# Eight PSUM banks in the head and VectorE for the residual's scaling, with a reordered router stage

## The chip, the cores and the metric

The kernel runs on 1 core of one Trainium2 chip. The metric is the device time of one execution in microseconds (us), lower is better. Three runs of the kernel before gave 830.20, 831.35 and 834.64 us; the median is 831.35.

## The reference

One layer over 16 learned meta tokens and 512 real tokens of width 1024. All matrix products are float32-exact to the tolerance, which the kernel reaches with three reduced products per float32 one.

```python
h = layer_norm(concat(meta_tokens, x), ln_in_g, ln_in_b)          # 528 x 1024
p = h @ w_in                                                      # all projections
(q_m, k_m, v_m, o_m, i_pre, f_pre, q_a, c_kv, q_idx, k_idx, w_idx, g_m, g_a) = split(p)
h_m = head_norm(mlstm(silu(conv(q_m, k_m)), v_m, i_pre, f_pre)) * mnorm_g * sigmoid(o_m)
h_a = sparse_attention(q_a, rms_norm(c_kv), q_idx, k_idx, w_idx)  # top 128 keys per query
y = sigmoid(g_m) * (h_m @ w_branch_m) + sigmoid(g_a) * (h_a @ w_branch_a)
h = layer_norm(2**0.25 * h + y @ w_out, ln1_g, ln1_b)
scores = sigmoid(h @ w_router)                                    # 16 experts, 4 groups
# best group by its top two scores, the two best experts of it, normalised weights
moe = sum over chosen e: weight * (silu(h @ w_gate[e]) * (h @ w_up[e])) @ w_down[e]
return layer_norm(2**0.25 * h + moe, ln2_g, ln2_b)[:, 16:]
```

## The kernel before, in words

Every engine has one hand-written instruction stream; the streams meet only in counting semaphores (`q[...]`), and an engine works its stream strictly in order. A step helper adds a wait of an engine on its own instruction.

A float32 operand is split into a high part (ScalarE, a copy to float32r) and a low part (VectorE, the difference), and `product` (lines 1066 to 1068) issues high x high, high x low and low x high. Weights come in 1 MB units: SyncE loads a unit into one of three `raw` slots, ScalarE's `split_hi` (line 681) and VectorE's `split_lo` (line 1582) split it. In the expert stage the same is done with twelve `m_raw` slots and three split slots (`m_split_hi` line 938, `m_split_lo` line 1864).

**The head.** SyncE issues the relative-bias table and a one-hot matrix, then the four token tiles `xn`, the meta tile `xm`, the gains `lng`, `lnb`, and weights. TensorE first multiplies the table by the one-hot matrix (lines 1097, 1098) into PSUM, ScalarE copies it out to `ftab` and stores it. VectorE takes means and variances per tile (lines 1596 to 1598), GpSimd the power (line 545), ScalarE normalises (line 690). TensorE transposes (line 1104) four of the eight 128-column groups `c` of each tile into banks 4 to 7; the other four groups (line 1110) follow later, each when the bank of group `c - 4` has been emptied (`lo_x`). Per group, ScalarE and VectorE apply gain and shift and make the two parts: for even `c` ScalarE writes `tmpT` (line 703) and the high part (705), for odd `c` ScalarE writes the high part straight from PSUM (698) and VectorE makes `tmpT` (1612); VectorE makes the low part (1613). The meta tile goes the same way in one piece (lines 1114, 1616, 1617, 707, 1619). The projections start when both parts of everything are there:

```python
pe.wait_ge(q["hi_x"], KC + 1)
pe.wait_ge(q["lo_x"], KC + 1)
```

**The residual.** The normalised tokens are also wanted later, with gain and bias, in token layout. GpSimd multiplies `xn` by the broadcast gain `gbc` and adds `bbc` (lines 566, 567), tile by tile, once all ten late loads (`load_late`, of which `kvg` is the last issued) and all transposes are through; SyncE stores each tile (line 424) and only then loads weight unit 4. ScalarE waits for all four stores before it squares the latent keys (line 729, whose output tile `md` lies on `xn`'s memory).

**The first projections.** TensorE works, in order, unit 0 (lines 1066 to 1068, twice 528 tokens), one half of unit 1, transposes of the latent keys (line 1148), the other half of unit 1, then a wait for VectorE's `c_tok` (line 1631) before four small transposes (line 1153) and unit 2. `c_tok` needs the squares (729), VectorE's `css` (1624), GpSimd's power and, in VectorE's order, `split_lo(2)`.

**The router stage.** After the output projection, tile `i` of `h1` is normalised by VectorE (line 1885), transposed by TensorE (`turned(i)`, line 1386), copied out by ScalarE (line 949) and multiplied by the router's weights (`router(i)`, line 1393). TensorE's order is `router(0), turned(2), router(1), turned(3), router(2), router(3)`. ScalarE splits `m_hi` units 0 and 1 before it copies tile 3 out. Then ScalarE's sigmoid (line 964), VectorE's choice of experts (lines 1898 to 1924), ranks (line 1421), lists (lines 1951, 1461), a gather of the first expert's tokens by GpSimd, its transposition (line 1441, all eight groups, `xe_done`), the split in `xe_hi` (ScalarE, line 970) and `xe_lo` (VectorE, line 1929), and the first expert's units.

In both kernels the loop over experts and the closing stage are the same.

## Time and profile before

| | |
|---|---|
| median of three runs | 831.35 us |
| the profiled execution's own time | 831.14 us |
| its span, first to last instruction | 829.1 us |
| what lies around the span | 2.0 us |
| TensorE busy | 760.9 us, 92% of the span |
| VectorE busy | 591.1 us, 71% |
| ScalarE busy | 431.7 us, 52% |
| GpSimd busy | 100.3 us, 12% |
| granted TensorE clock, mean | 0.970 |

The span is the time from the first to the last instruction on the core. Busy shares are means over stages with different limits, so each stage has to be read by itself. PE is TensorE, PEld its weight load, DVE VectorE, ACT ScalarE, POOL GpSimd, SPq and ACTq the instructions of SyncE and ScalarE that issue DMAs.

### The profile page before, as it was taken

To read this page: it belongs to the slowest core of one execution; us is meant where nothing else is said; L and a number is where in the kernel's file an instruction comes from. 1 tells how busy PE (TensorE), PEld (TensorE's weight loads), DVE (VectorE), ACT (ScalarE), POOL (GpSimd) and SP (SyncE) were. 2 spreads that over 40 slices of the span, in tenths; PEclk is the share of its full clock that TensorE was granted. 3 is DMA by queue.
4 is the path that set the end of the run, shared out by engine and by line. 5 is a ranking of instruction groups with operands and counts; after the bars stand their busy time and mean duration, and the time that the engine had idled before them with its cause. 6 is when DMAs were issued, how large, how long until landed. Compare 5 with 4: busy or idle time off the path is not lost.

```text
span 829.1 us, 10885 instructions
## 1 busy us (share of the span) xinstructions
PE 760.9 (92%) x4024; PEld 612.9 (74%) x4026; DVE 591.1 (71%) x797; ACT 431.7 (52%) x506; POOL 100.3 (12%) x116
## 2 busy tenths in 40 slices
PE   3399999999899899999999868899999999999993
PEld 1296799897467577787888766688888888888872
DVE  4905999797226644542464867889898989898978
ACT  4433333343642544573232032577888777878745
POOL 5540000000001000000000201212111111112001
PEclk9999999999999899999999977999999999999997
DMA  8645222321055111135237973799999999999162
GB/s 201 202 131 195 89 84 70 103 58 44 0 180 220 61 52 52 51 106 171 81 104 257 407 251 106 254 328 409 399 398 397 395 399 396 391 402 397 61 249 102
DMA packets 102469, 171.09 MB, mean 206 GB/s; under 512 B 18760, under 2 KB 39496, under 8 KB 102368
## 3 DMA queue, kind: packets, MB, share of 16 engines
q1 hardware_dynamic: 95672, 151.82, 51.5%
q0 software_dynamic: 4608, 12.92, 4.0%
q10 hardware_dynamic: 2152, 5.85, 1.8%
q8 instruction: 24, 0.39, 0.2%
q14 instruction: 13, 0.11, 0.0%
HBM read 160.26 MB, written 21.09 MB: 219 GB/s over the span
## 4 chain that ended last, share of the span: by engine, by line
PE 83%; DVE 9%; issue 3%; ACT 3%; SPq 1%; DMA 1%; POOL 0%; DVEq 0%; ACTq 0%; POOLq 0%
PE low L1066 15%; PE low L1068 15%; PE low L1067 15%; PE wide L1066 7%; PE wide L1068 7%; PE wide L1067 7%; PE wide L1441 2%; PE low L1236 1%; PE low L1336 1%; PE low L1298 1%; PE wide L1221 1%; PE low L1393 1%; PE wide L1269 1%; PE wide L1454 1%; SPq L407 1%
## 5 line engine op out<-in xcount | busy, mean ns | idle before, releaser
L1864 DVE TENSOR_TENSOR m_lo<-m_raw,m_hi 128x2048 fp32r<-128x2048 f32 x95 | 215.0, 2290 | 30.9 <-ACT m_hi L938 30.2
L938 ACT ACTIVATE m_hi<-m_raw 128x2048 fp32r<-128x2048 f32 x95 | 179.8, 1918 | 24.8 <-PE low L1068 24.0
L1066 PE MATMUL low<-m_hi,xe_hi 128*128 128x512 f32 x256 | 103.4, 404 | 2.6 <-DVE xe_lo L1929 1.5
L1066 PE MATMUL low<-hT_hi,w_hi 128*128 128x512 f32 (+1 forms) x240 | 95.6, 398 | 10.6 <-issue 10.6
L1068 PE MATMUL low<-m_hi,xe_lo 128*128 128x512 f32 x256 | 100.7, 393 | 0.0
L1067 PE MATMUL low<-m_lo,xe_hi 128*128 128x512 f32 x256 | 100.2, 392 | 0.0
L1582 DVE TENSOR_TENSOR w_lo<-raw,w_hi 128x2048 fp32r<-128x2048 f32 x28 | 64.1, 2290 | 45.7 <-ACT w_hi L681 45.5
L1067 PE MATMUL low<-hT_lo,w_hi 128*128 128x512 f32 (+1 forms) x240 | 93.4, 389 | 0.0
L1068 PE MATMUL low<-hT_hi,w_lo 128*128 128x512 f32 (+1 forms) x240 | 92.7, 386 | 0.0
L681 ACT ACTIVATE w_hi<-raw 128x2048 fp32r<-128x2048 f32 x28 | 53.5, 1910 | 17.6 <-PE wide L1068 8.3
L1066 PEld LDWEIGHTS low<-hT_hi,w_hi 128*128 128x128 f32 x240 | 46.8, 195 | 20.3 <-issue 11.0
L1066 PEld LDWEIGHTS low<-m_hi,xe_hi 128*128 128x128 f32 x256 | 48.5, 189 | 15.7 <-DVE m_lo L1864 4.4
L1068 PEld LDWEIGHTS low<-m_hi,xe_lo 128*128 128x128 f32 x256 | 48.3, 189 | 10.7
L1067 PEld LDWEIGHTS low<-m_lo,xe_hi 128*128 128x128 f32 x256 | 48.6, 190 | 9.3
L1068 PEld LDWEIGHTS low<-hT_hi,w_lo 128*128 128x128 f32 x240 | 46.8, 195 | 9.2
L1067 PEld LDWEIGHTS low<-hT_lo,w_hi 128*128 128x128 f32 x240 | 46.9, 195 | 8.6 <-issue 0.2
L1066 PE MATMUL wide<-m_hi,hd_hi 128*128 128x512 f32 x128 | 51.4, 402 | 1.4 <-DVE hd_lo L1938 1.4
L1068 PE MATMUL wide<-m_hi,hd_lo 128*128 128x512 f32 x128 | 50.1, 391 | 0.0
L1067 PE MATMUL wide<-m_lo,hd_hi 128*128 128x512 f32 x128 | 49.8, 389 | 0.0
L970 ACT ACTIVATE xe_hi<-wide 128x1024 fp32r<-128x1024 f32 x16 | 16.4, 1027 | 45.5 <-PE wide L1441 45.5
L1066 PE MATMUL wide<-hT_hi,w_hi 128*128 128x264 f32 x128 | 36.9, 288 | 1.1 <-ACT relu L759 1.0
L1067 PE MATMUL wide<-hT_lo,w_hi 128*128 128x264 f32 x128 | 36.3, 283 | 0.0
(370 smaller groups left out, 1465.8 us busy)
## 6 DMA issues: line engine op xcount, KB each, us to landing
m_raw<-in_w_gate SPq DMA_DIRECT2D x32, 1024.0 KB, 8.9
m_raw<-in_w_up SPq DMA_DIRECT2D x32, 1024.0 KB, 8.3
m_raw<-in_w_down SPq DMA_DIRECT2D x31, 1024.0 KB, 9.5
raw<-in_w_in SPq DMA_DIRECT2D x19, 1024.0 KB, 5.3
raw<-in_w_out SPq DMA_DIRECT2D x4, 1024.0 KB, 5.0
y<-y_dram SPq DMA_DIRECT2D x8, 512.0 KB, 6.9
table_dram<-table_row ACTq DMA_DIRECT2D x1, 2624.0 KB
strips<-table_dram SPq DMA_DIRECT2D x8, 264.0 KB, 4.3
```

The costliest lines, as they stand in the source:

```text
L407: sp.dma_start(unit3(raw, u % RAW, u)[:, :, to:to + n], src).then_inc(raw_loaded[u % RAW], 16)
L681: nc.scalar.activation(w_hi[:, u % SPL, :], raw[:, u % RAW, :], ACT.Copy).then_inc(q["hi_ready"], 1)
L938: nc.scalar.activation(m_hi[n % MS][:, :], (m_spare if is_last(n, j) else m_raw[slot])[:, :], ACT.Copy).then_inc(q["m_hi_ready"], 1)
L970: nc.scalar.activation(xe_hi[:, :, :], wide[1][:, :].rearrange("p (c x) -> p c x", c=KC), ACT.Copy).then_inc(q["xe_hi_ready"], 1)
L1066: nc.tensor.matmul(outp, lh, rh, start=first, stop=False)
L1067: nc.tensor.matmul(outp, lh, rl, start=False, stop=False)
L1068: return nc.tensor.matmul(outp, ll, rh, start=False, stop=last)
L1221: mm = nc.tensor.matmul(o, kT[:, h, META + j * P:META + (j + 1) * P], qT[:, h, META + j * P:T], start=True, stop=True)
L1236: mm = nc.tensor.matmul(oo, dw[:, g % 2, lo:lo + P], v_ext[:, j, g, :], start=False, stop=(j == i))
L1441: mm = nc.tensor.transpose(wide[1][:, c * P:(c + 1) * P], xg[slot][:, c * P:(c + 1) * P], ident[:, :])
L1582: v.tensor_tensor(w_lo[:, u % SPL, :], raw[:, u % RAW, :], w_hi[:, u % SPL, :].bitcast(F32), ALU.subtract).then_inc(q["lo_ready"], 1)
L1864: v.tensor_tensor(m_lo[n % MS][:, :], (m_spare if is_last(n, j) else m_raw[n % MR])[:, :], m_hi[n % MS][:, :].bitcast(F32), ALU.subtract). ...
```

## The change

**Head.** The table product, its copy and its store move from the front to after unit 1 (ScalarE copies it out before `split_hi(3)`); the loads of table and one-hot matrix move behind the first weights and the two broadcast rows. All eight groups of each tile are transposed at once, into banks 4, 5, 6, 7, 0, 1, 2, 3; the meta tile's transposes go to bank 4 after `lo_x` is 1. ScalarE does groups 0 and 1 before `split_hi(0)`. GpSimd builds two masks between the powers of the first tiles. The eight scaling instructions go from GpSimd to VectorE, after `split_lo(1)`. ScalarE's squares write into `score` and no longer wait for the stores. `side_done` and `side_out` replace six signals (`kv_done`, `ckv_done`, `table_done`, and `kv_out`, `fabs_ready`, `table_out`) and count to three each.

**Router stage.** `turned(2)` goes ahead of `router(0)`; a float32 product of 512 columns whose result nobody reads follows `router(0)` and `turned(3)`; unit 1's two splits go behind the sigmoid (ScalarE) and behind `slots_of(2, 8)` (VectorE); the split of the first expert's tokens is done in two halves of 512 columns, and the first expert unit waits for the first half only.

```diff
 (SyncE)
-            sp.dma_start(relb[:, :], a["rel_bias"]).then_inc(q["table_in"], 16)
-            sp.dma_start(oneh[:, :], onehot).then_inc(q["table_in"], 16)
             for i in range(TT):
                 sp.dma_start(xn[:, i, :], a["x"][0, i * P:(i + 1) * P, :]).then_inc(x_loaded[i], 16)
...
             load(1)
+            sp.dma_start(gbc[:, :], bcast_rows(a["ln_in_g"], D)).then_inc(q["load_late"], 16)
+            sp.dma_start(bbc[:, :], bcast_rows(a["ln_in_b"], D)).then_inc(q["load_late"], 16)
+            sp.dma_start(relb[:, :], a["rel_bias"]).then_inc(q["table_in"], 16)
+            sp.dma_start(oneh[:, :], onehot).then_inc(q["table_in"], 16)
...
-            sp.dma_start(gbc[:, :], bcast_rows(a["ln_in_g"], D)).then_inc(q["load_late"], 16)
-            sp.dma_start(bbc[:, :], bcast_rows(a["ln_in_b"], D)).then_inc(q["load_late"], 16)
 (GpSimd)
-            pool.wait_ge(q["load_late"], 16 * 10)
-            pool.wait_ge(q["xt_done"], KC)
-            for i in range(TT):
-                pool.wait_ge(q["xn_ready"], i + 1)
-                step(nc.gpsimd.tensor_tensor(xn[:, i, :], xn[:, i, :], gbc[:, :], ALU.mult))
-                nc.gpsimd.tensor_tensor(xn[:, i, :], xn[:, i, :], bbc[:, :], ALU.add).then_inc(q["h_ready"], 1)
-                pool.wait_ge(q["h_ready"], i + 1)
 (ScalarE)
-            act.wait_ge(q["table_done"], 1)
-            nc.scalar.activation(ftab[:, :], wide[0][0:AH, 0:FX], ACT.Copy).then_inc(q["table_out"], 1)
-            act.wait_ge(q["table_out"], 1)
-            act.dma_start(table_row, ftab[:, :]).then_inc(q["table_put"], 16)
...
-            split_hi(0)
             act.wait_ge(q["load_consts"], 16 * 2)
             for c in range(KC):
+                if c == 2:
+                    split_hi(0)
                 act.wait_ge(q["xt_done"], c + 1)
...
-            act.wait_ge(q["h_stored"], 16 * TT)
...
-                square = nc.scalar.activation(md[0:n, 0:R], src, ACT.Square, accum_out=css[0:n, i:i + 1])
+                square = nc.scalar.activation(score[0:n, 0:R], src, ACT.Square, accum_out=css[0:n, i:i + 1])
...
             evac(B_QI + 1, qidxT[:, 1, :])
+            act.wait_ge(q["side_done"], 3)
+            nc.scalar.activation(ftab[:, :], wide[0][0:AH, 0:FX], ACT.Copy).then_inc(q["side_out"], 1)
+            act.wait_ge(q["side_out"], 3)
+            act.dma_start(table_row, ftab[:, :]).then_inc(q["table_put"], 16)
             split_hi(3)
+            act.wait_ge(q["h_stored"], 16 * TT)
...
             m_split_hi(0)
-            m_split_hi(1)
             store_h1(3)
             turned_out(3)
...
+            m_split_hi(1)
             m_split_hi(MS - 1)
...
-            xe_hi_out(0)
+            act.wait_ge(q["xe_done"], 1)
+            for half, done in ((0, "xe_half_hi"), (1, "xe_hi_ready")):
+                nc.scalar.activation(xe_hi[:, 4 * half:4 * half + 4, :], bank[6 + half][:, :].rearrange("p (c x) -> p c x", c=4), ACT.Copy).then_inc(q[done], 1)
 (TensorE)
             for i in range(TT):
                 pe.wait_ge(q["xn_ready"], i + 1)
-                for c in range(4):
-                    mm = nc.tensor.transpose(bank[4 + c][:, i * P:(i + 1) * P], xn[:, i, c * P:(c + 1) * P], ident[:, :])
+                for c in range(KC):
+                    mm = nc.tensor.transpose(bank[(4 + c) % 8][:, i * P:(i + 1) * P], xn[:, i, c * P:(c + 1) * P], ident[:, :])
                     if i == TT - 1:
                         mm.then_inc(q["xt_done"], 1)
-            for c in range(4, KC):
-                pe.wait_ge(q["lo_x"], c - 3)
...
             by_channel(take(B_QI + 1)[:, :], 1, P, META, T).then_inc(q["block_done"], 1)
+            pe.wait_ge(q["table_in"], 32)
+            nc.tensor.matmul(wide[0][0:AH, 0:512], relb[:, :], oneh[:, 0:512], start=True, stop=True)
+            nc.tensor.matmul(wide[0][0:AH, 512:FX], relb[:, :], oneh[:, 512:FX], start=True, stop=True).then_inc(q["side_done"], 1)
             pe.wait_ge(q["c_ready"], TT + 1)
...
+            def idle_product():
+                nc.tensor.matmul(bank[1][:, :], ident[:, :], g1[:, 0:512], start=True, stop=True)
             pe.wait_ge(q["late_consts"], 16 * 8)
+            turned(2)
             router(0)
-            turned(2)
+            idle_product()
             router(1)
             turned(3)
+            idle_product()
             router(2)
             router(3)
...
-            pe.wait_ge(q["xe_lo_ready"], 1)
             for u in range(4):
+                pe.wait_ge(q["xe_lo_ready" if u else "xe_half_lo"], 1)
 (VectorE)
             split_lo(1)
+            dve.wait_ge(q["load_late"], 16 * 10)
+            for i in range(TT):
+                step(v.tensor_tensor(xn[:, i, :], xn[:, i, :], gbc[:, :], ALU.mult))
+                v.tensor_tensor(xn[:, i, :], xn[:, i, :], bbc[:, :], ALU.add).then_inc(q["h_ready"], 1)
             dve.wait_ge(q["css_ready"], 1)
...
-            for u in range(MS - 1):
-                m_split_lo(u)
+            m_split_lo(0)
...
             slots_of(2, 8)
+            m_split_lo(1)
             m_split_lo(MS - 1)
-            xe_lo_out(0)
+            for half, ready, done in ((0, "xe_half_hi", "xe_half_lo"), (1, "xe_hi_ready", "xe_lo_ready")):
+                dve.wait_ge(q[ready], 1)
+                v.tensor_tensor(xe_lo[:, 4 * half:4 * half + 4, :], bank[6 + half][:, :].rearrange("p (c x) -> p c x", c=4),
+                                xe_hi[:, 4 * half:4 * half + 4, :].bitcast(F32), ALU.subtract).then_inc(q[done], 1)
```

## Rows read from the trace of the kernel before

**Rows 1.** The page: the chain that ended last, by engine.
```profile
PE 83%; DVE 9%; issue 3%; ACT 3%; SPq 1%; DMA 1%; POOL 0%; DVEq 0%; ACTq 0%; POOLq 0%
```
**Rows 2.** Waits of TensorE, whole span: who waited for whom, us, times, longest.
```profile
PE low L1066 <- issue: 10.6, 1, 10.6
PE low L1153 <- DVE c_tok L1631: 2.0, 1, 2.0
PE low L1448 <- DVE hid L1934: 1.5, 1, 1.5
```
**Rows 3.** Timeline of VectorE, 26 to 42 us: start, duration, instruction, count, idle before.
```profile
26.42 1.50 DVE L1613 TENSOR_TENSOR hT_lo<-tmpT,hT_hi 128x512 fp32r<-128x512 f32 x2
28.74 3.44 DVE L1613 TENSOR_TENSOR hT_lo<-tmpT,hT_hi 128x512 fp32r<-128x512 f32 x2
32.94 1.99 DVE L1613 TENSOR_TENSOR hT_lo<-tmpT,hT_hi 128x512 fp32r<-128x512 f32 x1
34.85 0.28 DVE L1616 TENSOR_TENSOR tmpM<-low,lng 128x128 f32<-128x128 f32 x1
35.16 2.11 DVE L1617 TENSOR_TENSOR tmpM<-tmpM,lnb 128x128 f32<-128x128 f32 x1
37.65 2.05 DVE L1619 TENSOR_TENSOR hT_lo<-tmpM,hT_hi 128x128 fp32r<-128x128 f32 x1 [0.38 <-ACT hT_hi L707]
39.62 2.28 DVE L1582 TENSOR_TENSOR w_lo<-raw,w_hi 128x2048 fp32r<-128x2048 f32 x1
```
**Rows 4.** Timeline of GpSimd, 28 to 52 us.
```profile
29.19 2.44 POOL L566 TENSOR_TENSOR xn<-xn,gbc 128x1024 f32<-128x1024 f32 x1 [8.38 <-DMA kvg<-in_kv_norm_g]
39.63 4.50 POOL L566 TENSOR_TENSOR xn<-xn,gbc 128x1024 f32<-128x1024 f32 x1
```
**Rows 5.** Timeline of the head, 0 to 40 us, all engines.
```profile
0.81 0.40 SPq L395 DMA_DIRECT2D relb<-in_rel_bias  x1
1.72 1.94 SPq L398 DMA_DIRECT2D xn<-in_x  x4
10.77 1.09 PE L1104 MATMUL wide<-ident,xn 128*128 128x128 f32 x4 [5.00 <-ACT xn L690]
17.38 1.91 ACT L681 ACTIVATE w_hi<-raw 128x2048 fp32r<-128x2048 f32 x1 [1.80 <-DMA raw<-in_w_in]
19.20 0.76 ACT L703 ACTIVATE tmpT<-wide,lnb,lng 128x512 f32<-128x512 f32 x1
19.99 0.63 ACT L705 ACTIVATE hT_hi<-tmpT 128x512 fp32r<-128x512 f32 x1
20.53 0.76 ACT L698 ACTIVATE hT_hi<-wide,lnb,lng 128x512 fp32r<-128x512 f32 x1
39.80 0.56 PE L1066 MATMUL low<-hT_hi,w_hi 128*128 128x264 f32 x1 [10.56 <-issue]
```
**Rows 6.** Timeline of VectorE, after the head.
```profile
62.14 0.17 DVE L1624 TENSOR_SCALAR css<-css 128x4 f32<-128x4 f32 x1 [20.24 <-ACT md L729]
```
**Rows 7.** Windows: stretch and length, busy us per engine (count), granted clock, DMA share, GB/s.
```profile
68.00:72.00 4.00, 4.00 (x11) 3.12 (x12) 3.86 (x5) 0.01 (x1) 0.00 (x0) 0.58 0.93 298
72.00:76.00 4.00, 4.00 (x18) 3.25 (x18) 3.75 (x5) 0.60 (x1) 0.00 (x0) 0.99 0.53 199
469.00:473.00 4.00, 1.49 (x14) 1.25 (x13) 3.44 (x5) 0.44 (x1) 1.46 (x1) 1.00 1.04 411
484.60:491.20 6.60, 6.50 (x34) 6.39 (x32) 4.31 (x3) 2.44 (x3) 0.00 (x0) 0.53 0.69 247
```
**Rows 8.** The chain of waits in the router stage: start, length, instruction, count.
```profile
478.79 1.69 PE low L1393 x16
484.80 6.32 PE low L1393 x32
```
**Rows 9.** Timeline of VectorE before the first expert's units.
```profile
510.43 1.22 DVE L1929 TENSOR_TENSOR xe_lo<-wide,xe_hi 128x1024 fp32r<-128x1024 f32 x1 [2.96 <-ACT xe_hi L970]
```
**Rows 10.** The chain of waits in the closing stage.
```profile
805.69 1.72 PE wide L1558 x4
```

More of the change, by code:

```diff
@@ L546, in _ @@
                 pool.wait_ge(q["rstd_ready"], i + 1)
+                if i == 0:
+                    step(nc.gpsimd.memset(tri_qs[:, :], 0.0))
+                    step(nc.gpsimd.affine_select(out=tri_qs[:, :], in_=tri_qs[:, :], compare_op=ALU.is_ge, fill=NOT_CAUSAL,
+                                                 base=0, pattern=[[-1, P]], channel_multiplier=1))
+                elif i == 1:
+                    step(nc.gpsimd.memset(tri_st[:, :], 0.0))
+                    step(nc.gpsimd.affine_select(out=tri_st[:, :], in_=tri_st[:, :], compare_op=ALU.is_ge, fill=NEG_MASK,
+                                                 base=0, pattern=[[1, P]], channel_multiplier=-1))
             for h in range(MH):
                 step(nc.gpsimd.tensor_copy(sel_row[64:68, h, :], ident[64:68, 64 + h:65 + h].to_broadcast([MH, P])))
-            step(nc.gpsimd.memset(tri_qs[:, :], 0.0))
-            step(nc.gpsimd.affine_select(out=tri_qs[:, :], in_=tri_qs[:, :], compare_op=ALU.is_ge, fill=NOT_CAUSAL,
-                                         base=0, pattern=[[-1, P]], channel_multiplier=1))
-            step(nc.gpsimd.memset(tri_st[:, :], 0.0))
-            step(nc.gpsimd.affine_select(out=tri_st[:, :], in_=tri_st[:, :], compare_op=ALU.is_ge, fill=NEG_MASK,
-                                         base=0, pattern=[[1, P]], channel_multiplier=-1))
             step(nc.gpsimd.memset(mask[:, 0:P], 0.0))
@@ L702, in _ @@
                     act.wait_ge(q["lo_x"], c - 1)
-                step(nc.scalar.activation(tmpT[:, c % 2, :], bank[4 + c % 4][:, :], ACT.Identity,
+                step(nc.scalar.activation(tmpT[:, c % 2, :], bank[(4 + c) % 8][:, :], ACT.Identity,
                                           bias=lnb[:, c:c + 1], scale=lng[:, c:c + 1]))
@@ L714, in _ @@
             act.wait_ge(q["block_out"], 1)
-            act.wait_ge(q["kv_done"], 1)
-            nc.scalar.activation(in_halves(cT[:, :]), both_halves(low[1][:, :]), ACT.Copy).then_inc(q["kv_out"], 1)
+            act.wait_ge(q["side_done"], 1)
+            nc.scalar.activation(in_halves(cT[:, :]), both_halves(low[1][:, :]), ACT.Copy).then_inc(q["side_out"], 1)
             act.wait_ge(q["load_late"], 16 * 10)
@@ L720, in _ @@
             step(nc.scalar.activation(rows[96:100, 0, :], rows[96:100, 0, :], ACT.Exp, scale=-1.0))
-            nc.scalar.activation(rows[96:100, 0, :], rows[96:100, 0, :], ACT.Ln, bias=1.0).then_inc(q["fabs_ready"], 1)
-            act.wait_ge(q["ckv_done"], 1)
+            nc.scalar.activation(rows[96:100, 0, :], rows[96:100, 0, :], ACT.Ln, bias=1.0).then_inc(q["side_out"], 1)
+            act.wait_ge(q["side_done"], 2)
             act.wait_ge(q["const_done"], 1)
-            act.wait_ge(q["h_stored"], 16 * TT)
             for i in range(TT + 1):
@@ L1094, in by_token @@
                 return mm
-            pe.wait_ge(q["table_in"], 32)
-            nc.tensor.matmul(wide[0][0:AH, 0:512], relb[:, :], oneh[:, 0:512], start=True, stop=True)
-            nc.tensor.matmul(wide[0][0:AH, 512:FX], relb[:, :], oneh[:, 512:FX], start=True, stop=True).then_inc(q["table_done"], 1)
-            pe.wait_ge(q["table_out"], 1)
             pe.wait_ge(q["const_done"], 1)
@@ L1120, in _ @@
             all_tokens(low[0], 0, 0).then_inc(q["block_done"], 1)
-            all_tokens(low[1], 0, R).then_inc(q["kv_done"], 1)
+            all_tokens(low[1], 0, R).then_inc(q["side_done"], 1)
             def channel_unit(u, b):
@@ L1156, in _ @@
             pe.wait_ge(q["block_out"], B_QI + 2)
+            pe.wait_ge(q["side_out"], 3)
             index_scores(0)
@@ L1611, in _ @@
                         dve.wait_ge(q["lo_x"], c - 1)
-                    step(v.tensor_scalar(tmpT[:, 1, :], bank[4 + c % 4][:, :], lng[:, c:c + 1], lnb[:, c:c + 1], ALU.mult, ALU.add))
+                    step(v.tensor_scalar(tmpT[:, 1, :], bank[(4 + c) % 8][:, :], lng[:, c:c + 1], lnb[:, c:c + 1], ALU.mult, ALU.add))
                 v.tensor_tensor(hT_lo[:, c, META:T], tmpT[:, c % 2, :], hT_hi[:, c, META:T].bitcast(F32), ALU.subtract).then_inc(q["lo_x"], 1)
@@ L1615, in _ @@
             wide_c = lambda t: t[:, :].rearrange("p (c o) -> p c o", o=1).to_broadcast([P, KC, META])
-            step(v.tensor_tensor(tmpM[:, :, :], bank[2][:, 0:KC * META].rearrange("p (c x) -> p c x", c=KC), wide_c(lng), ALU.mult))
+            step(v.tensor_tensor(tmpM[:, :, :], bank[4][:, 0:KC * META].rearrange("p (c x) -> p c x", c=KC), wide_c(lng), ALU.mult))
             v.tensor_tensor(tmpM[:, :, :], tmpM[:, :, :], wide_c(lnb), ALU.add).then_inc(q["affine_m"], 1)
```

25 lines of the change are left out of this document (11 added, 14 removed).

## The prediction

> **What bounds the kernel now.** I read first the chain that ended last: TensorE has 83% of it, VectorE 9% [rows 1]. So a change pays only where TensorE stands still or runs slowly. The waits of TensorE then say where: one of 10.6 us before the first projection, put down to "issue" because two VectorE and ScalarE signals end it together, 2.0 us for `c_tok`, 1.5 us for the first expert's `hid` [rows 2]. The first is by far the longest, and everything after it hangs on it: the projections begin at 39.80 [rows 5].
>
> What fills the head is in the timelines of VectorE and GpSimd side by side. An `hT_lo` difference takes 0.75 us (two in 1.50). From 28.74 on, two take 3.44 and the last takes 1.99; the add into `tmpM` over 128 columns takes 2.11 and the last `hT_lo`, as small, 2.05, where its neighbour L1616, which reads one operand from PSUM, takes 0.28 [rows 3]. These stretched ones lie in the time in which GpSimd scales the residual, from 29.19 on [rows 4]. The reverse is there too: at 39.62 VectorE's `w_lo` starts first and takes its plain 2.28, and GpSimd's product, begun at 39.63, takes 4.50 instead of 2.44 [rows 3, 4]. The two engines take turns for whole instructions when both have two operands in SBUF. The granted clock of TensorE comes last: 0.58 from 68 to 72 us and 0.53 from 484.6 to 491.2 [rows 7], at 1.2 GHz for most of both.
>
> **The head.** Four terms.
> (a) Two loads leave SyncE's front. The first token tile was issued at 1.72 and can go at 0.81 [rows 5]: 0.9 us. The statistics are VectorE's own back to back work behind the first tile, so all of it moves.
> (b) Order of the first groups. The first tile's transposes start at 10.77 - 0.9 = 9.9. Now there are 32 of them ahead of the end, four in 1.09 [rows 5], so 0.27 each, and the last tile's eight begin at 9.9 + 24 x 0.27 = 16.4; group 0 is whole at 16.7. ScalarE does groups 0 and 1 (0.76 + 0.63 + 0.76, 2.2 with gaps) to 18.9 and then splits unit 0 (1.91) to 20.8, whose weights had landed at 17.4 [rows 5] and come no later. VectorE's `w_lo` (2.28) ends at 23.1. Before, ScalarE split first, from 17.38, did groups 0 and 1 to 21.3, then VectorE made group 1's 0.8 + 0.75 and `w_lo` to about 25.0. So VectorE passes this point 1.9 us earlier, the 0.9 of (a) included.
> (c) From there VectorE and ScalarE pass the groups back and forth as before. Without GpSimd's instructions beside them the stretched ones fall to their plain length: 3.44 to 1.50, 1.99 to 0.75, 2.11 to 0.28, 2.05 to 0.28: 1.9 + 1.2 + 1.8 + 1.8 = 6.7 us. GpSimd keeps memsets, copies and masks, over before 20 us.
> (d) The eight banks take the waits of the later transposes away; they were no longer than VectorE's own queue, so nothing more. The meta tile's transposes wait for group 0 alone: nothing.
> Head: 1.9 + 6.7 = 8.6 us; the first projection starts at 31.2. Bounds: 7.5 (one of the slow instructions has another reason) to 9.5 (transposes faster, below).
>
> The Trainium skill, SBUF — State Buffer, section "Who interferes with whom", says that a VectorE instruction with two SBUF inputs and a GpSimd instruction that reads SBUF exclude each other for the whole instruction, and that one with at most one SBUF input isn't held. The 0.28 beside the 2.11 [rows 3] agrees. By that rule only GpSimd's own reading counts: (c) would be whole, and the eight scaling instructions on VectorE hold nobody, since GpSimd then has nothing to read.
>
> **What moves into cover.** VectorE's scaling: eight instructions of 128x1024. `w_lo` has twice the columns and takes 2.28 [rows 3], so 1.14 plus 0.1 for the step: 10 us. They stand behind `split_lo(1)` (31.2 + 1.9 for the high part + 2.3 = 35.4), so they last to 45.4. Behind them in VectorE's queue is `css`, for which VectorE stood idle 20.24 us until 62.14 [rows 6]; 8.6 earlier that is 53.5. So 8 us are left, and they cost nothing. If the cover were gone, each us would be one of `c_tok` and of TensorE. Their own wait, for all ten late loads, ended at 29.19 before [rows 4] and is in time; the order change in SyncE's queue (two rows ahead, two small loads more) adds under 1 us to it. SyncE stores the four tiles by about 48.5 and then loads unit 4, some 3.5 us sooner than before: nothing. ScalarE's squares don't wait for the stores; they waited for TensorE's transposes before, so nothing. The table's product on TensorE (656 columns; 512 take 0.86, two in 1.72 [rows 10], so 1.1 us) falls in the 2.0 us in which TensorE waits for `c_tok` [rows 2]: `c_tok` comes from ScalarE and VectorE and keeps its distance, so the product costs nothing and 0.9 us of waiting is left. ScalarE's copy of it (0.7) and the wait for its store stand before unit 3's high part and before `qaT`; both have some 5 us of idle time there. Bound if not: 0.7 us. Six signals on two counters: no instruction less, nothing.
>
> **The clock after `c_tok`.** After the 2.0 us of waiting, the clock fell and 11 products ran between 68 and 72 where 18 run between 72 and 76 [rows 7]: 7 products of 0.22, 1.6 us lost. With 0.9 us of idle time and a product before it, I expect the clock to stay: 1.6 us won. Against it: at 469 to 473 TensorE worked only 1.49 of 4.00 us and the clock stayed at 1.00 [rows 7], so whether it falls depends on more than the length of one pause. Bounds 0 and 1.7. I take 1.6.
>
> **The router stage.** TensorE from 478.8: `turned(2)` 1.1 (eight transposes at the full clock take what four do at half), `router(0)` 1.7 [rows 8], idle product 0.86 [rows 10], `router(1)` 1.7, `turned(3)` 1.1, at 485.2; the second idle product to 486.1; `router(2)` and `router(3)` 1.7 each to 489.5. ScalarE's copy of tile 3, now in front of unit 1's split, is ready 1.1 after 485.2 and isn't waited for. Before: 484.80 + 6.32 = 491.12, since the last 32 records ran at half clock (16 took 1.69 before, 32 take 6.32 [rows 8]). So 1.6 won if the clock stays to the end; if it falls where it fell before, the second idle product takes 1.7 and the sum is 485.2 + 1.7 + 6.3 = 493.2: 2.1 lost. I think that it stays through the idle products and falls late in the last 3.4 us: 1.2 won.
> Behind it VectorE gets 2.3 us more before the first expert's tokens (unit 1's low part); it stood idle 2.96 us there [rows 9], so it's hidden, with 0.6 left. The halves: before, 1.03 for the high part and 1.22 for the low [rows 9], 2.3 in all. Now the first half is ready after 0.6 + 0.7, so TensorE starts 1.0 sooner; but VectorE, whose queue then ends in `hid`, for which TensorE waits 1.5 [rows 2], is through only 0.2 sooner (0.6 + 0.6 + 0.1 + 0.7 against 2.3). So 0.2 counts. Bounds of the stage: -2.1 and +2.6. Taken: 1.2 + 0.2 = 1.4. Unit 1's slot comes free some 17 us later, and its reload with it; a slot's contents are used more than 30 us after, so nothing.
>
> **Sum.** 8.6 + 1.6 + 1.4 = 11.6 us off the profiled execution's own 831.1 (span 829.1 and 2.0 around it): 819.5. The median of the runs shown is 831.35, so the two are one scale. I forecast 819.5, 1.4% faster. The experts and the closing stage start earlier and are otherwise as before: TensorE is busy through and pulls its weights along.
>
> **Rivals.**
> 1. The clock gives nothing at either place: 8.6 + 0.2 us: 822.3. For it: the fall in rows 7 has a pause that is only halved, and the router's products are short. 0.22.
> 2. The transposes warm TensorE. The 32 of the head follow each other without a pause for 8.7 us, and the projections from 39.80 reach the full rate after some microseconds of work. If they do so too, the last tile's are ready 0.8 us sooner, and with everything else as forecast 818.7. 
> 3. The stretched VectorE rows have another cause than GpSimd (the broadcast loads of `gbc`, `bbc` land at that time): then only 1.9 + 1.6 + 1.4 is won less 1 for the same slowness in the scaling: 827.2. Against it: the 0.28 between two stretched rows and GpSimd's 4.50. 0.05.
> 4. A later stage takes it back: from 100 to 200 us VectorE's top-k selection is nearly as full as TensorE, and a pause falls at a worse moment for the clock several times. Each fall costs 1.6 us; four of them and a us of waiting give 826. 0.06.
> 5. Slower than before: VectorE's scaling stands in front of `css`. It decides once the last late load lands after 43.5; each us later is one us for `c_tok`, the projections and all behind. To eat the 11.6 it has to land at 55 or later, at 60 the time is 836. The load's neighbours in SyncE's queue landed by 29.19 [rows 4]. 0.03.
> Forecast: 0.52.
>
> **How the numbers follow.** Changes of this kernel within 0.5% (4.2 us) can't be told from none: faster means under 827.2. Forecast, 1, 2 and half of 4 are faster: 0.89. Rival 3 and half of 4: 0.08 the same. Rival 5: 0.03. The range: the forecast's own goes from 8.6 + 1.6 + 2.6 with 0.8 and a us of noise (816) to a head of 7.5 with nothing from the clock (823.6). That also covers rivals 1 and 2; 816 to 823.6 leaves out rivals 3 to 5 and little else.
>
> **What would show it.** Right: the first L1066 product at 31.2, every L1613 at 0.7 to 0.8 and L1617, L1619 at 0.3; eight 1.2 us instructions on VectorE and `css` still preceded by idle time; 0.9 us before the `smallT` transposes and 0.23 between the products of unit 2; the sigmoid's idle time ended at a distance of 11 us from the end of the output projection instead of 12.5, and a granted clock near 1 until 486 minus the head's gain. Wrong: slow small VectorE instructions with GpSimd idle; `css` without idle time before it; a clock of 0.5 from `turned(3)` on; a first projection after 33 us, which would cost the forecast most.

## The result, and the profile after

The changed kernel takes 818.86 us (median of 4 runs, 816.62 to 819.72) against 830.78 for the kernel before in the same job (828.96 to 834.64): a ratio of 0.985, 95% interval 0.981 to 0.989. The forecast was 819.5 us, with a range of 816.0 to 823.6. The profiled execution took 818.94 us, of which 817.2 are its span, so 12.2 us less than the one of before.

The chain that ended last, by engine (answers to [rows 1]):
```profile
PE 84%; DVE 10%; ACT 3%; issue 2%; DMA 0%; POOL 0%; DVEq 0%; ACTq 0%; POOLq 0%
```
TensorE is still the bound. Its waits (engine, tile, line, what it waited for, us, times, longest; answers to [rows 2]):
```profile
PE low L1061 <- DVE hT_lo L1617: 11.2, 1, 11.2
...
PE low L1061 <- DVE m_lo L1865: 1.7, 1, 1.7
...
PE low L1446 <- DVE hid L1934: 1.5, 1, 1.5
```
The wait before the first projection is no shorter than before (11.2 against 10.6), since the transposes in front of it end sooner too. The length of a wait doesn't show the gain; its end does. VectorE's timeline shows that end (start, duration, instruction, count, idle before; answers to [rows 3] and [rows 6]):
```profile
4.21 1.42 DVE L1594 BATCH_NORM_STATS2 stats<-xn 128x6 f32<-128x512 f32 x2 [4.21 <-DMA xn<-in_x]
...
19.16 2.29 DVE L1580 TENSOR_TENSOR w_lo<-raw,w_hi 128x2048 fp32r<-128x2048 f32 x1 [0.26 <-ACT w_hi L675]
...
25.13 1.44 DVE L1611 TENSOR_TENSOR hT_lo<-tmpT,hT_hi 128x512 fp32r<-128x512 f32 x2
...
27.39 0.69 DVE L1611 TENSOR_TENSOR hT_lo<-tmpT,hT_hi 128x512 fp32r<-128x512 f32 x1
28.00 0.28 DVE L1614 TENSOR_TENSOR tmpM<-wide,lng 128x128 f32<-128x128 f32 x1
28.32 0.29 DVE L1615 TENSOR_TENSOR tmpM<-tmpM,lnb 128x128 f32<-128x128 f32 x1
28.98 0.29 DVE L1617 TENSOR_TENSOR hT_lo<-tmpM,hT_hi 128x128 fp32r<-128x128 f32 x1 [0.38 <-ACT hT_hi L697]
...
32.99 1.22 DVE L1621 TENSOR_TENSOR xn<-xn,gbc 128x1024 f32<-128x1024 f32 x1
...
41.42 1.22 DVE L1622 TENSOR_TENSOR xn<-xn,bbc 128x1024 f32<-128x1024 f32 x1
52.18 0.17 DVE L1625 TENSOR_SCALAR css<-css 128x4 f32<-128x4 f32 x1 [9.54 <-ACT score L718]
```
Every stretched row is down to its plain length, and the eight scaling instructions (32.99 to 42.64) are followed by 9.5 us of idle time: they lie in cover. TensorE's timeline of the head (answers to [rows 5]):
```profile
9.37 1.09 PE L1095 MATMUL wide<-ident,xn 128*128 128x128 f32 x4 [9.37 <-ACT xn L679]
10.25 1.06 PE L1095 MATMUL low<-ident,xn 128*128 128x128 f32 x4
...
14.80 0.64 PE L1095 MATMUL wide<-ident,xn 128*128 128x128 f32 x4
15.28 0.60 PE L1095 MATMUL low<-ident,xn 128*128 128x128 f32 x4
...
29.37 0.56 PE L1061 MATMUL low<-hT_hi,w_hi 128*128 128x264 f32 x1 [11.21 <-DVE hT_lo L1617]
29.73 0.42 PE L1062 MATMUL low<-hT_lo,w_hi 128*128 128x264 f32 x1
```
Four transposes take 1.06 to 1.11 until the last tile, whose four take 0.60 to 0.64: TensorE has risen to 2.4 GHz while it did nothing but transposes. (The durations say so. The column of the granted clock reads 1.00 from the start of the trace to its first fall and can't be used here.) The projections then start 0.22 apart, at 1.2 GHz again after 11.2 us of idle time.

Around `c_tok`, the same engine (the wait of 2.0 us in [rows 2]):
```profile
55.54 1.02 PE L1139 MATMUL wide<-oneh,relb 32*8 32x512 f32 x2
56.41 0.40 PE L1140 MATMUL wide<-oneh,relb 32*8 32x144 f32 x2
57.62 0.41 PE L1143 MATMUL low<-ident,smallT 8*128 8x8 f32 x4 [0.81 <-DVE c_tok L1632]
...
59.62 0.63 PE L1061 MATMUL low<-hT_hi,w_hi 128*128 128x512 f32 x1
```
The table product fills the wait and 0.81 is left. But the products from 59.2 to 62.6 are 0.43 apart, not 0.23: the clock fell all the same. The windows say it in another way (stretch, length, busy time and count of PE, PEld, DVE, ACT, POOL, granted clock, DMA share, GB/s; answers to [rows 7]):
```profile
60.00:64.00 4.00, 4.00 (x13) 3.13 (x12) 3.79 (x7) 0.17 (x1) 0.00 (x0) 0.67 0.34 116
...
474.00:478.00 4.00, 4.00 (x33) 3.52 (x33) 2.43 (x3) 1.67 (x2) 0.00 (x0) 1.00 0.66 264
478.00:482.00 4.00, 2.00 (x15) 1.89 (x14) 1.43 (x7) 1.96 (x3) 0.00 (x0) 0.64 0.88 272
```
In the router stage it stayed at 1.00 up to 478 and fell near 479. The chain of waits there (start, length, what; answers to [rows 8]) has the idle products at L1403:
```profile
470.03 1.69 PE low L1384 x16
471.72 0.95 PE low L1403 x2
472.67 1.69 PE low L1384 x16
474.37 0.92 PE wide L1377 x8
475.28 0.86 PE low L1403 x2
476.14 3.87 PE low L1384 x32
```
The last 32 router records take 3.87 instead of 6.32 [rows 8]. And the halves of the first expert's tokens on VectorE (answers to [rows 9]), with the wait of the first unit on TensorE:
```profile
498.49 1.27 DVE L1978 TENSOR_TENSOR xe_lo<-wide,xe_hi 128x512 fp32r<-128x512 f32 x2
```
```profile
499.22 0.50 PE L1061 MATMUL low<-m_hi,xe_hi 128*128 128x512 f32 x1 [0.88 <-DVE xe_lo L1978]
...
510.45 0.47 PE L1061 MATMUL low<-m_hi,xe_hi 128*128 128x512 f32 x1 [1.71 <-DVE m_lo L1865]
```

(`xe_lo` is the low part of the expert's tokens, `m_lo` that of a weight unit.) Where the time came from, by the start of the same work in the two timelines (us from the start of each span):

| point | before | after | sooner |
|---|---|---|---|
| first projection | 39.80 | 29.37 | 10.4 |
| `smallT` transposes behind `c_tok` | 67.58 | 57.62 | 10.0 |
| first index scores | 80.82 | 70.83 | 10.0 |
| end of the output projection | 478.63 | 468.99 | 9.6 |
| sigmoid | 491.14 | 480.04 | 11.1 |
| first expert unit | 511.71 | 499.22 | 12.5 |
| first `hid` transposes | 527.71 | 515.81 | 11.9 |
| transposes of the next expert's tokens | 541.51 | 528.02 | 13.5 |
| last expert done (`yl_hi`) | 803.09 | 791.12 | 12.0 |
| end of the span | 829.1 | 817.2 | 11.9 |

### The profile page after: what moved, and what is told of

The parts are those of the page before. It is cut to its first block, busy times and chain, and to the rows that moved or that the text cites. A ratio compares the mean times of both kernels' runs of the same rounds, so it can differ in the third digit from the quotient of the medians.

```text
span 817.2 us, 10896 instructions
## 1 busy us (share of the span) xinstructions
PE 754.8 (92%) x4030; PEld 609.8 (75%) x4030; DVE 593.6 (73%) x806; ACT 431.9 (53%) x507; POOL 78.2 (10%) x108
## 4 chain that ended last, share of the span: by engine, by line
PE 84%; DVE 10%; ACT 3%; issue 2%; DMA 0%; POOL 0%; DVEq 0%; ACTq 0%; POOLq 0%
PE low L1061 15%; PE low L1062 15%; PE low L1063 15%; PE wide L1061 7%; PE wide L1063 7%; PE wide L1062 7%; PE wide L1439 1%; PE low L1227 1%; DVE slots L1951 1%; DVE m_lo L1865 1%; PE low L1327 1%; PE wide L1212 1%; PE low L1289 1%; ACT w_hi L675 1%; PE wide L1260 1%
## 5 line engine op out<-in xcount | busy, mean ns | idle before, releaser
L931 ACT ACTIVATE m_hi<-m_raw 128x2048 fp32r<-128x2048 f32 x95 | 179.6, 1917 | 23.1 <-PE low L1063 22.6
L1061 PE MATMUL low<-hT_hi,w_hi 128*128 128x512 f32 (+1 forms) x240 | 95.8, 399 | 11.2 <-DVE hT_lo L1617 11.2
L1063 PE MATMUL wide<-hT_hi,w_lo 128*128 128x264 f32 x128 | 36.2, 283 | 0.0
```

What stands on the lines that cost most here:

```text
L931: nc.scalar.activation(m_hi[n % MS][:, :], (m_spare if is_last(n, j) else m_raw[slot])[:, :], ACT.Copy).then_inc(q["m_hi_ready"], 1)
L1061: nc.tensor.matmul(outp, lh, rh, start=first, stop=False)
L1063: return nc.tensor.matmul(outp, ll, rh, start=False, stop=last)
```

## The experiments

All were timed in five rounds beside the kernel before (medians 831.56, 831.23 and 830.41 in the three jobs). `a1` is an edit of the kernel before, the others of the changed kernel. The points of the table are measured in each experiment's own profile, one per kernel.

**a1_scale_only: the kernel before with nothing but the scaling moved to VectorE.**
```diff
-            pool.wait_ge(q["load_late"], 16 * 10)
-            ... (GpSimd's loop over the tiles)
+            dve.wait_ge(q["load_late"], 16 * 10)
+            for i in range(TT):
+                step(v.tensor_tensor(xn[:, i, :], xn[:, i, :], gbc[:, :], ALU.mult))
+                v.tensor_tensor(xn[:, i, :], xn[:, i, :], bbc[:, :], ALU.add).then_inc(q["h_ready"], 1)
```

> The kernel before with one edit: the eight scaling instructions of the residual move from GpSimd to VectorE, behind the split of unit 1. Theory (the two engines exclude each other while both read two operands from SBUF): the four stretched VectorE instructions fall to 0.7 and 0.3 us, the first projection starts at 33.0 instead of 39.8, and the time is 831 - 7 = 824 us. Rival (the broadcast loads or something else stretch them): they stay at 2 us with GpSimd idle, the first projection stays at 39.8, 831 us.

Measured: 823.54 us (820.54 to 824.95), ratio 0.990 (0.987 to 0.992). VectorE's timeline:
```profile
28.91 1.44 DVE L1605 TENSOR_TENSOR hT_lo<-tmpT,hT_hi 128x512 fp32r<-128x512 f32 x2
...
31.17 0.69 DVE L1605 TENSOR_TENSOR hT_lo<-tmpT,hT_hi 128x512 fp32r<-128x512 f32 x1
31.78 0.28 DVE L1608 TENSOR_TENSOR tmpM<-low,lng 128x128 f32<-128x128 f32 x1
32.10 0.29 DVE L1609 TENSOR_TENSOR tmpM<-tmpM,lnb 128x128 f32<-128x128 f32 x1
32.77 0.29 DVE L1611 TENSOR_TENSOR hT_lo<-tmpM,hT_hi 128x128 fp32r<-128x128 f32 x1 [0.38 <-ACT hT_hi L699]
```
All four kinds of stretched rows are plain again, with every load where it was, and the first projection starts at 33.16, 6.6 us sooner. So GpSimd was the cause, not the loads beside it. Both the time and the start came out as expected.

**a2_scale_pool: the changed kernel with the scaling back on GpSimd** (the same edit the other way round).

> The changed kernel with the scaling given back to GpSimd, all else kept. My record says that the move is worth 6.7 us: then the first projection starts at about 36 and the time is 825 to 826. Rival, which the changed kernel's trace suggests: GpSimd can begin only when the last late load has landed, at about 29.3, and the reordered head is through at 29.4 by then, so only the last small instruction and the split of unit 1 can be stretched; the first projection starts at 29.4 to 31.5 and the time is 819 to 821.

Measured: 819.20 us (816.95 to 821.19), ratio 0.985 (0.983 to 0.988): the same as the changed kernel. The first projection starts at 29.56. GpSimd's and VectorE's timelines say why:
```profile
30.43 2.38 POOL L568 TENSOR_TENSOR xn<-xn,gbc 128x1024 f32<-128x1024 f32 x1 [11.41 <-DMA kvg<-in_kv_norm_g]
32.88 4.31 POOL L569 TENSOR_TENSOR xn<-xn,bbc 128x1024 f32<-128x1024 f32 x1
```
```profile
29.17 0.29 DVE L1625 TENSOR_TENSOR hT_lo<-tmpM,hT_hi 128x128 fp32r<-128x128 f32 x1 [0.38 <-ACT hT_hi L705]
30.97 3.98 DVE L1588 TENSOR_TENSOR w_lo<-raw,w_hi 128x2048 fp32r<-128x2048 f32 x1 [1.51 <-ACT w_hi L683]
```
GpSimd starts when the late loads have landed, at 30.43, and VectorE has finished the head at 29.46. The two still collide, in unit 1's `w_lo` (3.98 instead of 2.29), but TensorE's first projections don't wait for that one. (The late loads also end 1.2 us later than in the kernel before, 30.43 against 29.19, since their order was changed.) In the changed kernel, then, the move of the scaling is worth nothing, and the orders alone bring 10.2 us at the first projection. Each of the two is enough by itself to keep the head out of GpSimd's way; their gains overlap and don't add.

**a3_router_before: the changed kernel with the router stage and the first expert's tokens as before** (order of `turned` and `router`, no idle products, one split of 1024 columns, unit 1's splits back in front).

> The changed kernel with the whole router stage of the kernel before (order of transposes, no idle products, unit 1 split early, tokens split in one piece). Theory: from the end of the output projection to the sigmoid 12.5 us instead of 11.0, the granted clock 0.5 during the last two router products, and the first expert's second phase 2.3 us later by the difference of the two traces: 821.0 us. Rival (the stage gives nothing because VectorE sets the pace behind it): 819 us.

Measured: 820.47 us (819.23 to 820.92), ratio 0.987 (0.984 to 0.989). From the end of the output projection to the sigmoid 12.4 us, as before (12.5; changed kernel 11.05), and to the first expert unit 33.1 us against 30.2. At the transposes of the next expert's tokens its stage has cost 3.9 us (63.0 against 59.0); the whole span is only 1.5 longer (818.7), since its output projection ended 0.7 sooner and a later fall of the clock, told of under Rival 4 below, is missing from its profile.

**a4_no_idle: the changed kernel without the two idle products.**
```diff
             router(0)
-            idle_product()
...
             turned(3)
-            idle_product()
```

> The changed kernel without the two idle products. Theory (they hold the clock): it falls to 0.5 near the third tile's transposes, the last two router products take 6.3 us instead of 3.9, 2.4 lost and 1.7 saved: sigmoid 0.7 us later than in the changed kernel, 819.6 us. Rival (the order of transposes alone keeps the clock): both products' 1.7 us are saved, or as much of it as tile 3's wait allows, some 1 us: 818 us.

Measured: 821.47 us (819.35 to 822.72), ratio 0.988 (0.986 to 0.990). The chain of waits:
```profile
472.75 6.14 PE low L1384 x32
```
TensorE's timeline, just in front of them:
```profile
471.66 1.09 PE L1377 MATMUL wide<-ident,h 128*128 128x128 f32 x8 [0.57 <-DVE h L1884]
```
Without the idle products the last 32 records are back at 6.14, and the sigmoid comes 12.35 after the output projection, 1.3 more than in the changed kernel. So of the 1.46 gained up to the sigmoid all but 0.16 is the idle products'; the third tile's earlier turn does next to nothing alone. They do two things at once: they put wide products between the narrow ones, and they fill the 0.57 us for which TensorE waits there without them (0.61 in the kernel before). Which of the two holds the clock no run separates. I had expected 819.6 us, 1.9 less than measured. A second fall of the clock came back with it, 40 us later, in the windows of this kernel (first row) and of the changed one (second):
```profile
516.00:520.00 4.00, 3.44 (x10) 2.80 (x11) 3.66 (x4) 3.01 (x3) 0.00 (x0) 0.70 0.95 376
```
```profile
516.00:520.00 4.00, 3.44 (x17) 2.72 (x17) 3.68 (x3) 3.46 (x3) 0.31 (x1) 1.00 1.02 386
```
With as many busy us, 10 products run instead of 17, and from `hid` to the next expert's tokens it takes 1.6 longer. This went the same way in every profile of the study: 13.8 to 13.9 us from `hid` to the next tokens in all four without idle products (the kernel before, `a1`, `a3`, `a4`), 12.2 in the ten with them. How products near 473 keep the clock up at 517 no run tells. The sigmoid came 12.4 to 12.6 us after the output projection in those four and 11.05 to 11.6 in the ten, so the gain of 1.46 is the upper end of what the idle products bring.

**b4_four_banks: the changed kernel with the transposes of before** (four groups ahead, then one by one as banks come free, `bank[4 + c % 4]`).

> The changed kernel with the transposes of the kernel before: four groups per tile into banks 4 to 7, the other four groups later into the same banks, the meta tile's into bank 2. All other orders are the changed kernel's. Theory (my record's term d, the eight banks are worth nothing): the later transposes are ready before ScalarE asks for them, and group 0 is whole 0.7 us sooner since only four transposes stand ahead of it per tile; the first projection starts between 28.7 and 29.4 and the time is 818 to 819. Rival (the eight banks are what shortened the head): the first projection at 31 or later, 820.5 or more.

Measured: 816.85 us (815.46 to 822.53), ratio 0.984 (0.982 to 0.987). The first projection starts at 28.88, 0.5 sooner than in the changed kernel. ScalarE takes the first group at 14.72 instead of 15.22, since fewer transposes stand ahead of it, and everything behind keeps that distance. The eight banks bring nothing. That they cost this half us fits ScalarE's row, but the first projections of other kernels with eight banks and no edit in the head lie between 29.03 (`a3`) and 30.09 (`c4`), so 28.88 isn't clear of them. The median is more than 1 us under the range that I had expected (818 to 819).

**b1_warm_head: 19 products of 512 columns, whose result nobody reads, while TensorE waits for the head.**
```diff
+            for c, count in ((3, 8), (5, 3), (6, 3), (7, 3), (8, 2)):
+                pe.wait_ge(q["lo_x"], c)
+                for _ in range(count):
+                    nc.tensor.matmul(bank[5][:, :], hT_hi[:, 0, META:META + P], hT_hi[:, 0, META:T], start=True, stop=True)
```

> The changed kernel with 19 reduced products of 512 columns that nobody reads on TensorE in the head's last 7 us (8 once three groups have their low part, then 3, 3, 3 and 2 as the later ones come), in the pause before the first projection. Theory (the clock is low there because TensorE stood still): the first 25 or so products of 264 columns take 0.12 us instead of 0.22 and the gain is 2.3 us, 816.5. Rival (the products delay something or the clock isn't raised): 818.9 or more, the first projection later than 29.4.

Measured: 813.33 us (812.56 to 814.19), ratio 0.979 (0.977 to 0.980), the fastest of the study. TensorE's timeline:
```profile
22.09 6.79 PE L1106 MATMUL wide<-hT_hi 128*128 128x512 f32 x19 [3.85 <-DVE hT_lo L1615]
29.38 0.36 PE L1061 MATMUL low<-hT_hi,w_hi 128*128 128x264 f32 x1 [0.50 <-ACT hT_hi L697]
29.58 0.28 PE L1062 MATMUL low<-hT_lo,w_hi 128*128 128x264 f32 x1
```
The first projection starts at the same time (29.38), but the projections are 0.12 apart from the first on. The `smallT` transposes come at 54.91, 2.7 sooner. In its profile the clock stays up behind `c_tok` too, so that the first index scores are 4.3 sooner (66.57) and the span is 812.1. The median is 3.2 us under the 816.5 that I had expected. Of the 5.2 us by which the span is shorter, 2.7 are the products' own; 1.6 come from the clock behind `c_tok` and 1.6 from another fall, near 786 us, that its profile doesn't have; 0.8 are lost between the first index scores and the first expert unit. Whether the products bring the two stretches at full clock as well, or the profile met them by chance, isn't shown. And even the 2.7 depend on what is compared: from the first projection to the `smallT` transposes it takes 25.5 us with them, 28.2 in the changed kernel, but 26.9 in `a4`, `b4` and `c1`, where the clock rose sooner.

**b2_warm_ctok: three idle products behind the table product**, to fill the last 0.8 us before `c_tok`; **b3_warm_both**: both of these.

> The changed kernel with 3 reduced products of 512 columns behind the table's product, in the 0.8 us in which TensorE waits for c_tok. Theory (the pause and the narrow products around it let the clock fall at 59.3): the clock stays in more of the executions, unit 2's products take 0.23 throughout, up to 1.6 us gained, 817.3. Rival (the fall depends on when the pause meets the chip's own rhythm, not on 0.7 us of filling): 818.9, and the fall still in the trace.

> Both fillings together. Theory: the gains add, 2.3 + up to 1.6: 815 to 816.5. Rival: no better than the better of the two.

Measured: `b2` 815.36 us (811.99 to 817.48), ratio 0.980 (0.978 to 0.982); `b3` 814.81 us (812.71 to 815.19), ratio 0.980 (0.978 to 0.982). The window of `b2` that answers to the 0.67 of the changed kernel:
```profile
60.00:64.00 4.00, 4.00 (x19) 3.21 (x18) 3.87 (x5) 0.60 (x1) 0.00 (x0) 1.00 0.24 69
```
The clock stayed, and from the transposes to the index scores there are 11.65 us instead of 13.2: the 1.6 that I had forecast for this place. Both medians are under what I had expected, that of `b2` by 1.9 us. Both together bring nothing over `b1` alone, in whose profile the clock had stayed anyway. `b2` and `b3` also lose something later: from the first index scores to the end of the output projection they take 399.2 and 399.6 us, all others 397.7 to 398.2. A fall of the clock near 200 us lasts 6.8 us in these two and 3.4 in the others (granted clock 0.51 from 199.4 to 206.2 in `b3`, 0.75 in `b1`).

**c1_split_first: `split_hi(0)` back ahead of the first groups.** **c2_loads_front: the two loads back in front of the first token tile.**
```diff
+            split_hi(0)
             act.wait_ge(q["load_consts"], 16 * 2)
...
             for c in range(KC):
-                if c == 2:
-                    split_hi(0)
```

> The changed kernel with ScalarE's split of unit 0 ahead of groups 0 and 1, as before. Theory (the order of the groups is a term of its own): unit 0 has landed at about 16, the split ends near 18, groups 0 and 1 are through at 20 and VectorE's low part of unit 0 at 23; the first projection starts 1.5 to 2 us later than 29.4, the time is 820.5. Rival (the order makes no difference, the loads ahead of it did it all): 29.4, 818.9.

> The changed kernel with the loads of the table and of the one-hot matrix back at the very front of SyncE's queue; the table's product stays where the change put it. Theory (the first token tile waits for these two issues and their transfer): the statistics start at 5.6 instead of 4.2 and all of the head moves by that, first projection at 30.5 to 30.8, 820.2. Rival: something else sets the first tile's arrival, 4.2 and 818.9.

Measured: `c1` 819.62 us (817.80 to 820.89), ratio 0.986 (0.983 to 0.988); its first projection starts at 32.11, 2.7 later, which shows that the order of the first groups is worth something. The clock gave it back: it rose sooner after the first projection (1.4 us less to the `smallT` transposes) and stayed up behind `c_tok` (11.7 us to the index scores, 1.6 less). The start is later and the time shorter than I had expected. `c2` 818.53 us (817.31 to 818.87), ratio 0.984 (0.982 to 0.987). The statistics start at 5.61 instead of 4.21, so the two loads hold up the first tile by 1.4 us; but the transposes, starting later and closer together, reach the full clock after less of them, ScalarE's first group comes only 0.8 later (16.00), the first projection starts only 0.8 later (30.16), and the whole time can't be told from that of the changed kernel; both are under what I had expected, the time by 1.7.

**c3_best: the four banks of `b4` with 12 idle products before the first projection**, meant to take the best of both.

> The changed kernel with the transposes of the kernel before (four groups in banks 4 to 7, then the others) and with 12 reduced products that nobody reads in the last 4 us before the first projection. Theory: the earlier group 0 (0.5 us) and the full clock at the first projections (2.3 us) add: first projection at 28.9, 812.5. Rival: too few products to raise the clock, 816.5.

Measured: 816.41 us (815.34 to 817.26), ratio 0.982 (0.980 to 0.984): not the best, and 3.9 us over the 812.5 that I had expected. TensorE's timeline:
```profile
25.09 4.36 PE L1110 MATMUL low<-hT_hi 128*128 128x512 f32 x12
29.29 0.28 PE L1061 MATMUL low<-hT_hi,w_hi 128*128 128x264 f32 x1
```
The transposes of the four banks last until 25.1, so the idle products come late, run partly at 1.2 GHz and put the first projection 0.4 behind that of `b4` (28.88). The projections behind them run at full clock even so, and the `smallT` transposes come at 54.74, sooner than in `b1` (54.91). So the head isn't what `c3` lacks. In its profile it is the clock, which fell behind `c_tok` (13.2 us to the index scores; 11.65 in `b4` and 11.66 in `b1`): its span is 1.6 longer than that of `b1`. The medians are 3.1 apart, and the rest is open.

**c4_after_again: the changed kernel once more, unedited.**

> The changed kernel once more, unedited, on the same chip as the other three, as their measure: 818.9, within 1.5 us. What differs between its trace and the first one shows how much the clock's falls move between executions of one program.

Measured: 818.18 us (817.96 to 819.69), ratio 0.984 (0.982 to 0.986). In its profile the third token tile came 0.6 late, the first projection started at 30.09 (29.37 in the first profile), and the clock fell behind `c_tok` again. With `a3`, `a4` and `b2`, which don't touch the head either, its first projections lie between 29.03 and 30.09. So a head read from one profile is good to about 0.7 us either way, and the experiments that moved it by about as much, `b4` and `c2`, show no more than that the effect is small.

## Why the prediction came out right, step by step

The time was forecast at 819.5 and measured at 818.9; the profiled execution gave 12.2 where the sum had 11.6. Most mechanisms held, but that the sum came so close is luck: the head gave 1.8 more than its term, the router stage with the first expert's start 0.9 more, and a fall of the clock near 520 that the sum didn't have 1.6; the clock after `c_tok` gave 1.6 less, and 0.8 and 1.5 were lost before the output projection and in the experts. These cancel but for 0.4.

**The head: 8.6 forecast (bounds 7.5 to 9.5), 10.4 measured.** Out of the bounds.
- Step (c), the end of the mutual exclusion, was right in cause and size: 6.6 in `a1`, 6.7 forecast. Rival 3 (loads as the cause) is refuted by the same run. What the step had wrong is that it counted this as the gain of the scaling's move. `a2` shows that the change's orders would have cleared the head of GpSimd without it.
- Step (b) was too small. VectorE ended unit 0's `w_lo` at 21.45 where the forecast had 23.1. The pitch of the transposes was mis-sized: I took 0.27 each from "four in 1.09", which contains the lead-in of the first; by the starts in the timeline four take 0.85 to 0.97, 5.4 us for the 24 ahead of the last tile instead of 6.5. And the first tile came 1.4 sooner instead of 0.9 (with the two loads in front the statistics start at 5.61 in `c2` and at 5.17 in `a1`, without them at 4.21). From the end of `w_lo` to the first projection it then takes 7.92 in both `a1` and the changed kernel. With `a1` at 33.16 these orders brought 3.8 more.
- Rival 2 was true in its mechanism and not in its price. The last tile's transposes ran at 2.4 GHz, eight in 1.1 us instead of 1.9; but ScalarE takes the groups one after the other and needs the first of them first, so the rest of the head got nothing of it here; in `c2`, where the clock rose earlier, ScalarE's first group got 0.6. In `b4` every four transposes take 1.08 to 1.12, and its projections start sooner. The rule of the Trainium skill, TensorE: Matmul & The Clock Gate, section "What's actually happening", that activity releases the low rate, held here with transposes as the only activity.
- Step (d): `b4` confirms that the eight banks bring nothing.

**Between the head and the output projection: 0.8 lost, nothing forecast.** 0.5 goes before `c_tok`: the projections ran 0.22 apart for 5.9 us in the changed kernel (29.37 to 35.23) and for 4.8 us in the one before (39.80 to 44.56). That isn't a rule of the earlier start: in `b4` (28.88) and `a4` (29.95) the clock was up after some 3 us, in `c4` (30.09) after 6. `b1` takes this stretch away. The other 0.3, spread over 400 us, I have not placed.

**What moves into cover** was right everywhere: eight instructions of 1.22, ended at 42.6 (45.4 forecast), 9.5 us of idle time behind them (8 forecast), no cost by `a2`; the table product between 55.5 and 56.8, and 0.81 of waiting left (0.9 forecast).

**The clock after `c_tok`: +1.6 forecast, 0 in the profile.** This step failed in the trace I judge by. The pause was halved and the clock fell as before. In `c4` it fell again, in `a2`, `a3`, `c2` and `c3` too; in `a4`, `b4`, `b1` and `c1`, with no edit at that place either, it stayed. So with that pause it goes either way (it fell in 6 of 10 profiles), and about half of the 1.6 should have stood in the sum, as Rival 1 warned. `b2` and `b3`, which leave no pause, kept it, in one profile each.

**The router stage: 1.4 forecast (1.2 + 0.2).** The first part measured 1.46 at the sigmoid, with the clock falling late in the last two `router` groups, as taken (3.87 for what takes 3.4 at full clock); `a4` gives it to the idle products. The first expert unit gained another 1.4 (halves 1.0 forecast), of which `a4`, without idle products, keeps 0.75; no run separates the halves from the moved splits of unit 1. It lost 0.6 of it to the first `hid`, for which TensorE waits 1.5 as before: 0.8 kept, 0.2 forecast. A new wait of 1.7 for `m_lo` at 510.45, which I had not named, took part of it. What was missed altogether is the fall of the clock near 520 that the idle products also prevent: 1.6 more at the next tokens. That fits `a4`, which loses 2.6 us in its median against 818.9 and not 1.3.

**Rival 4** had a part: 1.5 of the 13.5 won by the next tokens are gone by the end of the last expert. No wait takes it: between these two points TensorE stands still once, for 1.41 us, in all 14 profiles. It is one more fall of the clock, in the last expert. TensorE's timeline, the changed kernel first, then the kernel before:
```profile
786.50 0.80 PE L1061 MATMUL wide<-m_hi,hd_hi 128*128 128x512 f32 x1 [1.41 <-DVE hd_lo L1938]
787.09 0.63 PE L1062 MATMUL wide<-m_lo,hd_hi 128*128 128x512 f32 x1
```
```profile
799.96 0.50 PE L1066 MATMUL wide<-m_hi,hd_hi 128*128 128x512 f32 x1 [1.41 <-DVE hd_lo L1938]
800.29 0.40 PE L1067 MATMUL wide<-m_lo,hd_hi 128*128 128x512 f32 x1
```
From 786.4 to 789.7 the granted clock is 0.50 and 8 products run; in the same stretch of the kernel before (799.9 to 803.2) it is 1.00 and 14 run. From the next tokens to `yl_hi` it takes 262.7 to 263.1 us in the six profiles that have this fall (the changed kernel, `c4`, `a2`, `a4`, `b4`, `c1`) and 261.2 to 261.6 in the eight that don't. No edit stands at that place, and what decides it no run tells. `b1` has no such fall and keeps all of its 17.0. (In the prediction this rival's own sum, four falls of 1.6 and a us, gives 826.9 and not 826, and the lower end of the range adds up to 816.5 and not 816. Nothing hangs on either.)

Added up over the profiled executions: head +10.4, up to the output projection -0.8, router stage +1.5, tokens and halves +0.8, clock near 520 +1.6, clock near 786 -1.5: 12.0, which is the span's 11.9 but for rounding.

## What to carry to other kernels

Where two engines exclude each other, ask when they meet before moving work: an order that brings one of them past the point in time is worth as much as the move, and the two gains don't add. Read the pitch of short TensorE instructions from the starts of neighbouring groups, not from a group's duration. TensorE, when it has to wait anyway, can be given wide products nobody reads, if they end before what it waits for arrives: here the kernel with them took 5 us less (813.3 against 818.2 and 818.9), of which its profile shows 2.7 at the place itself. And read the granted clock before you blame a wait: here two falls of it (behind `c_tok` and near 786), 1.5 or 1.6 us each, come and go between profiles of kernels with the same code at those places, so that a difference of two spans isn't yet the worth of an edit.

## What was not expected of the hardware

- The clock fell while TensorE was busy without a pause, in narrow products: in the changed kernel it fell near 479, in the last 32 router records, after more than 10 us without idle time. Without the two products of 512 columns (0.9 us each), and with a pause of 0.57 us, it fell earlier, and the 32 records took 6.14 instead of 3.87 (`a4`).
- With the same two products went the clock 40 us later, in 14 of 14 profiles, by a way that no run shows.
- A fall near 786 us was in 6 of 14 profiles and one near 200 us lasted 3.4 or 6.8 us, with the same instructions at both places.
- The clock rose during transposes alone after some 5 us of them (9.37 to 14.80), and in `c2` after 2.7 us (10.76 to 13.46).
- In a collision the engine that comes second waits for the whole instruction of the first: an instruction of VectorE of 2.29 took 3.98 behind GpSimd's, and GpSimd's next, plain 2.38, took 4.31 behind that one (`a2`).
